# Turning the scan rows of a state-space stage by DMA transposes in place of TensorE transposes

## The reference, cut to what matters

```python
y = ssd(xs, dt, a, bm, cm)                 # chunked scan: diagonal part + carried state
y = y + d_skip[:, None] * xs
y = y.reshape(bsz, s, SSM_D_INNER) * silu(z_ssm)
y = rms_norm(y per group of 512 columns) * ssm_norm_g
y_ssm = y @ w_branch_ssm                   # 2048 -> 1024 columns
merged = sigmoid(g_att) * y_att + sigmoid(g_ssm) * y_ssm
x = x + gate * (merged @ w_out)
```

## Time and profile before

| what | value |
|---|---|
| median of 3 runs | 2744.04 us (2742.4 to 2745.33) |
| span of the profiled execution | 2738.7 us |
| PE busy in the span | 2476.7 us (90%) |
| DVE busy | 1654.1 us (60%) |
| ACT busy | 1033.5 us (38%) |
| POOL busy | 629.3 us (23%) |
| scan stage of group 0 | about 1958 to 2071 us |
| scan stages of groups 1 to 3, first instruction of DVE | 2150.09, 2341.31, 2532.41 us |

### The profile page before, as it was taken

One profiled execution on the slowest core, in us unless ns is written; L12 is line 12 of the kernel. 1 busy time (PEld: TensorE's weight loads), 2 busy tenths in 40 slices (PEclk: granted clock), 3 DMA queues, 4 the chain that ended last, 5 costly groups with the idle time before them and its releaser, 6 DMA issues. The chain is left out here.

```text
span 2738.7 us, 40825 instructions
## 1 busy us (share of the span) xinstructions
PE 2476.7 (90%) x15855; PEld 1326.7 (48%) x15855; DVE 1654.1 (60%) x2961; ACT 1033.5 (38%) x1594; POOL 629.3 (23%) x618
## 2 busy tenths in 40 slices
PE   4999985989799997699789989898999999999999
PEld 3556543545455554355334446644454444444444
DVE  6787774322233233576499988754774766757864
ACT  5111452221122222555544348822443533624620
POOL 2021020000000001331345410000540731712702
PEclk9999997999899999799899999999999999999999
DMA  8685575899999998220112210053002002011133
GB/s 245 205 290 177 197 268 196 316 386 391 389 386 370 385 350 300 84 70 16 39 39 85 95 52 2 17 208 131 8 1 100 8 1 100 9 52 49 66 116 126
DMA packets 131570, 433.12 MB, mean 158 GB/s; under 512 B 27792, under 2 KB 37392, under 8 KB 122960
## 3 DMA queue, kind: packets, MB, share of 16 engines
q1 hardware_dynamic: 95536, 349.13, 35.0%
q10 hardware_dynamic: 25696, 48.93, 5.0%
q0 software_dynamic: 10176, 32.78, 4.0%
HBM read 371.86 MB, written 58.94 MB: 157 GB/s over the span
## 5 line engine op out<-in xcount | busy, mean ns | idle before, releaser
L1484 PE MATMUL m_gu<-conv_y,m_xT 128*64 128x256 f32 x1024 | 233.6, 388 | 17.8 <-DMA arena<-in_moe_w_up 15.5
L2604 POOL TENSOR_TENSOR group_words<-group_words 128x1024 f16<-128x1024 f16 x64 | 149.8, 2361 | 373.7 <-PE i_pj L144 364.4
L1486 PE MATMUL m_gu<-arena,m_xT 128*64 128x256 f32 x1024 | 233.6, 388 | 0.0
L1563 DVE TENSOR_TENSOR m_hid<-m_sg,m_gu 64x256 f32<-64x256 f32 x96 | 39.6, 412 | 318.2 <-ACT m_sg L1532 318.2
L1486 PEld LDWEIGHTS m_gu<-arena,m_xT 128*64 128x64 f32 x1024 | 143.1, 140 | 73.9 <-issue 15.4
L1532 ACT ACT_TABLE_LOAD x48 | 61.6, 1283 | 305.8 <-issue 293.1
L1506 PE MATMUL m_y_ps<-arena,m_hidT 128*64 128x512 f32 x768 | 175.4, 598 | 0.0
L1484 PEld LDWEIGHTS m_gu<-conv_y,m_xT 128*64 128x64 f32 x1024 | 143.1, 140 | 36.0 <-issue 25.0
L142 PE MATMUL s_pj<-hT,arena 128*128 128x512 f16 x384 | 147.4, 384 | 12.7 <-issue 11.6
L142 PE MATMUL i_pj<-hT,group_words 128*128 128x512 f16 x384 | 146.5, 381 | 13.5 <-DVE group_words L357 8.0
L143 PE MATMUL s_pj<-hT,arena 128*128 128x512 f16 x384 | 147.1, 383 | 0.0
(11 more groups left out here) (594 smaller groups left out, 6634.7 us busy)
## 6 DMA issues: line engine op xcount, KB each, us to landing
arena<-in_moe_w_down SPq DMA_DIRECT2D x32, 2048.0 KB, 24.9
conv_y<-in_moe_w_gate SPq DMA_DIRECT2D x22, 2048.0 KB
arena<-in_moe_w_up SPq DMA_DIRECT2D x22, 2048.0 KB
hT<-in_moe_w_gate SPq DMA_DIRECT2D x10, 2048.0 KB
hT<-in_moe_w_up SPq DMA_DIRECT2D x10, 2048.0 KB
x_tok<-in_ada_w ACTq DMA_DIRECT2D x8, 2048.0 KB, 12.6
slot_out<-m_y ACTq DMA_DIRECT2D x96, 128.0 KB
arena<-in_w_gates SPq DMA_DIRECT2D x24, 512.0 KB, 4.2
```

Of the source, the lines that this page charges most:

```text
L1484: g = nc.tensor.matmul(gu_ps[i][g_rows, 0:FFN // 2], lhsT=xT[:, c, :], rhs=k.wg[e % WEIGHT_SLOTS][:, c, cols], start=c == 0, stop=c == KC - 1)
L1486: u = nc.tensor.matmul(gu_ps[i][u_rows, 0:FFN // 2], lhsT=xT[:, c, :], rhs=k.wu[e % WEIGHT_SLOTS][:, c, cols], start=c == 0, stop=c == KC - 1)
L1563: nc.vector.tensor_tensor(hid[:, i, :], sg[:, i, :], gu_ps[i][u_rows, 0:FFN // 2], ALU.mult) \
L2604: return tuple(k.nc.gpsimd.tensor_tensor(k.y_U[:, t % 2, n], k.adt_parts[:, n, t, heads].unsqueeze(2).to_broadcast([P, HPG, P]), k.upto16. ...
```

## The change

ACT and DVE now make the two f16 parts of each row before it is turned, for the rows 0 to 6. They lie in the chunk's 512 f32 words of `x_ssm`, which are no longer needed then: 512 f16 columns of high part, 512 of low part. SP turns such a row with one DMA transpose of 128 x 1024 f16 straight into `yT`. Row 7 is still turned on TensorE and split after it. In the last group SP issues the merge loads behind its seven transposes.

```diff
+        rows16 = lambda t: k.x_ssm[:, t, :].bitcast(F16).rearrange("p (a n) -> p a n", a=2)
+        turned_in = [k.sem(f"y{g}_turned_in{i}") for i in range(2)]
...
+        def turn_rows(sp, t):
+
+            sp.wait_ge(q["row_low"], t + 1)
+            sp.dma_start_transpose(yT.rearrange("p a c s -> p (a c) s")[:, :, t * P:(t + 1) * P],
+                                   rows16(t).rearrange("p a n -> p (a n)")).then_inc(turned_in[t // 4], 16)
+
         if g + 1 == SSM_GROUPS:
...
                 sp.wait_ge(k.att_stored, 16 * KC)
+                for t in range(TT - 1):
+                    turn_rows(sp, t)
                 sp.wait_ge(q["z_done"], TT - EARLY_Z)
...
+                sp.wait_ge(turned_in[0], 16 * 4)
+                sp.wait_ge(turned_in[1], 16 * 3)
...
-            def transposes(t):
-
-                pe.wait_ge(q["normed"], t + 1)
-                if t:
-                    pe.wait_ge(q["tr_low"], t)
+            def last_turn():
+                pe.wait_ge(q["normed"], 1)
                 for c in range(4):
-                    last = nc.tensor.transpose(tr[:, c * P:(c + 1) * P], k.z_ssm[:, t, c * P:(c + 1) * P],
+                    last = nc.tensor.transpose(tr[:, c * P:(c + 1) * P], k.z_ssm[:, TT - 1, c * P:(c + 1) * P],
...
-                if j == 0 or j == KC:
-                    pe.wait_ge(q["tr_high"], 4 + a // P)
-                    pe.wait_ge(q["tr_low"], 4 + a // P)
+                if j == 0:
+                    pe.wait_ge(turned_in[0], 16 * 4)
+                elif j == KC:
+                    pe.wait_ge(turned_in[1], 16 * 3)
+                    pe.wait_ge(q["tr_high"], 1)
+                    pe.wait_ge(q["tr_low"], 1)
...
-                if t >= 2:
-                    transposes(t - 2)
+                if t == TT + 1:
+                    last_turn()
...
-                if t >= 2:
-                    act.wait_ge(q["tr_done"], t - 1)
-                    nc.scalar.copy(yT[:, 0, :, (t - 2) * P:(t - 1) * P],
-                                   tr[:, :].rearrange("p (c q) -> p c q", q=P)).then_inc(q["tr_high"], 1)
+                    if t < TT:
+                        act.wait_ge(q["rstd"], t)
+                        nc.scalar.activation(rows16(t - 1)[:, 0], k.z_ssm[:, t - 1, :], ACT.Copy,
+                                             scale=ss[:, t - 1:t]).then_inc(q["row_high"], 1)
...
-                if t - 1 in end:
-                    accumulate(dve, end[t - 1])
...
-                    step(v.reciprocal(ss[:, t - 1:t], ss[:, t - 1:t]))
+                    v.reciprocal(ss[:, t - 1:t], ss[:, t - 1:t]).then_inc(q["rstd"], 1)
+                if t == TT:
+                    dve.wait_ge(q["rstd"], TT)
                     v.tensor_scalar(k.z_ssm[:, t - 1, :], k.z_ssm[:, t - 1, :], ss[:, t - 1:t], None, ALU.mult) \
...
-                if t >= 2:
-                    dve.wait_ge(q["tr_high"], t - 1)
-                    h = yT[:, 0, :, (t - 2) * P:(t - 1) * P]
-                    v.tensor_tensor(yT[:, 1, :, (t - 2) * P:(t - 1) * P],
-                                    tr[:, :].rearrange("p (c q) -> p c q", q=P), h, ALU.subtract) \
-                        .then_inc(q["tr_low"], 1)
...
+                if t in end:
+                    accumulate(dve, end[t])
+                if 1 <= t < TT:
+                    dve.wait_ge(q["row_high"], t)
+                    v.scalar_tensor_tensor(rows16(t - 1)[:, 1], in0=k.z_ssm[:, t - 1, :], scalar=ss[:, t - 1:t],
+                                           in1=rows16(t - 1)[:, 0], op0=ALU.mult, op1=ALU.subtract) \
+                        .then_inc(q["row_low"], 1)
```

More of the change, by code:

```diff
@@ L2845, in ssm_scan_stage @@
         tr, br = k.ps(f"y{g}_tr", [P, HALF], ctx=ctx), k.ps(f"y{g}_br", [P, HALF], ctx=ctx)
+        rows16 = lambda t: k.x_ssm[:, t, :].bitcast(F16).rearrange("p (a n) -> p a n", a=2)
+        turned_in = [k.sem(f"y{g}_turned_in{i}") for i in range(2)]
         names = ("pool_in", "U_done", "seg_done", "cb_done", "E_done", "cbm_done", "M_done", "yd_done",
-                 "yo_done", "st_done", "state_done", "yo_read", "y_done", "gated", "squared", "std", "normed",
-                 "tr_done", "tr_high", "tr_low", "br_done", "br_out", "dve_step", "xd_done", "f_high", "f_low",
+                 "yo_done", "st_done", "state_done", "yo_read", "y_done", "gated", "squared", "std", "rstd",
+                 "row_high", "row_low", "normed", "tr_done", "tr_high", "tr_low", "br_done", "br_out", "dve_step", "xd_done", "f_high", "f_low",
                  "small", "z_done", "z_out")
@@ L3029, in _ @@
                                          scale=1.0 / GW).then_inc(q["std"], 1)
-                if t >= 2:
-                    act.wait_ge(q["tr_done"], t - 1)
-                    nc.scalar.copy(yT[:, 0, :, (t - 2) * P:(t - 1) * P],
-                                   tr[:, :].rearrange("p (c q) -> p c q", q=P)).then_inc(q["tr_high"], 1)
+                    if t < TT:
+                        act.wait_ge(q["rstd"], t)
+                        nc.scalar.activation(rows16(t - 1)[:, 0], k.z_ssm[:, t - 1, :], ACT.Copy,
+                                             scale=ss[:, t - 1:t]).then_inc(q["row_high"], 1)
+                if t == TT + 1:
+                    act.wait_ge(q["tr_done"], 1)
+                    nc.scalar.copy(yT[:, 0, :, (TT - 1) * P:], tr[:, :].rearrange("p (c q) -> p c q", q=P)) \
+                        .then_inc(q["tr_high"], 1)
             if g + 1 < SSM_GROUPS:
@@ L3101, in _ @@
                     dve.wait_ge(q["std"], t)
-                    step(v.reciprocal(ss[:, t - 1:t], ss[:, t - 1:t]))
+                    v.reciprocal(ss[:, t - 1:t], ss[:, t - 1:t]).then_inc(q["rstd"], 1)
+                if t == TT:
+                    dve.wait_ge(q["rstd"], TT)
                     v.tensor_scalar(k.z_ssm[:, t - 1, :], k.z_ssm[:, t - 1, :], ss[:, t - 1:t], None, ALU.mult) \
                         .then_inc(q["normed"], 1)
-                if t >= 2:
-                    dve.wait_ge(q["tr_high"], t - 1)
-                    h = yT[:, 0, :, (t - 2) * P:(t - 1) * P]
-                    v.tensor_tensor(yT[:, 1, :, (t - 2) * P:(t - 1) * P],
-                                    tr[:, :].rearrange("p (c q) -> p c q", q=P), h, ALU.subtract) \
-                        .then_inc(q["tr_low"], 1)
-            accumulate(dve, end[TT + 1])
+                if t == TT + 1:
+                    dve.wait_ge(q["tr_high"], 1)
+                    v.tensor_tensor(yT[:, 1, :, (TT - 1) * P:], tr[:, :].rearrange("p (c q) -> p c q", q=P),
+                                    yT[:, 0, :, (TT - 1) * P:], ALU.subtract).then_inc(q["tr_low"], 1)
+                if t in end:
[5 more added lines that the diff above has]
+                        .then_inc(q["row_low"], 1)
             for j in range(KC, 2 * KC):
```

## The result

The changed kernel takes 2754.66 us (median of 4 runs, 2752.74 to 2759.44), the kernel before 2743.61 beside it on the same chip: ratio 1.0044, 95% interval 1.0032 to 1.0056. So it is slower, by 11 us, where the forecast had 5.5. The profiled execution has a span of 2750.8 us, 12.1 above that of before. The stages ahead of the scan differ by a few us from execution to execution, so what follows goes by strides: from the first instruction of a group's scan stage on DVE (the memset of `eps`) to that of the next. Before, a stride is 191.1; after, 194.3. Each group pays 3.2 us.

The account below looks back on a forecast made before the run. The prediction took the ring of DVE and POOL, not TensorE, as the bound: +1.08 + 1.27 - 0.98 = +1.37 per group, +5.5 over four, 2749.5 us. Its own range was 2746 to 2753, the stated range 2736 to 2760.

Parts of the forecast that it names:

- four turns longer by 0.27: DVE's new operation costs 0.45, the dropped L3103 saves 0.18; four turns from chunk 1 to 5 add 1.08 us per group.
- L3088 (before: L3070) late in turn 5: In turn 5 DVE's state decay ends at 5.31 instead of 4.04 after y, making the first accumulate 1.27 us later.
- transposes of rows 5 and 6: Two sets of transposes on TensorE's dense path behind the second branch product go, gaining 2 x 0.49 = 0.98 us per group.
- the clock: TensorE's added idle time was charged nothing, since waits of 1.3 us stand in the trace before.
- The ring of DVE and POOL: In the scan turns DVE and POOL hand one shared resource to and fro, which sets the 10.09 us turn, not TensorE.
- The price of 0.45: Hold on the shared resource by DVE's new operation with two SBUF inputs, 0.45 us, bounds 0.18 and 0.60.
- The round trip over ACT: DVE waits each turn for ACT's 0.73 us copy; the delay is hidden in turns 1 to 4, not in turn 5.
- The transposes of turns 2 to 6: Five sets on TensorE before the second branch product turn into waiting for POOL's operand and the first accumulate: nothing gained.
- The new operation gets in ahead of L2616: Rival, chance 0.17: ACT's copy takes under 0.6 us, turn 5 costs 0.27, a group +0.37, time 2745.5.
- Rows land late: Rival, chance 0.16: from 8.3 us a DMA on, product 8 waits for row 6; 2753.5 at 8.8, near 2763 at 10.
- The ring shrinks: Rival, chance 0.12: the new operation holds nothing from POOL, five turns lose 0.18 each; -7.5 us, 2736.5.
- TensorE is the bound after all: Rival, chance 0.10: removing seven sets of transposes and the 1.3 us wait gains 4.7 us per group, time 2725.

Follow-up runs that it names:

- third run: Changed kernel with a memset to zero in place of the operation making the low parts of rows 0 to 6: 2743.66 us, ratio 1.0004 to the kernel before.
- second run: Changed kernel with row 4's low part computed in turn 6 behind the first accumulate, not in turn 5: 2740.93 us, ratio 1.0004 to the kernel before.
- sixth run: Changed kernel with branch products 1 and 3 put into the accumulator bank that the transposes left idle: 2738.33 us, ratio 0.9985 to the kernel before.
- ninth run: Changed kernel with idle bank used, row 4's low part later, and three filler passes behind the stage's last product: 2731.65 us, ratio 0.9965 to the kernel before.
- first run: Changed kernel with 18 unused TensorE passes filling the wait before product 1: 2750.99 us, ratio 1.0033 to the kernel before.
- seventh: Changed kernel with products 1 and 3 in the idle bank and row 4's low part behind the first accumulate: 2735.40 us, ratio 0.9970 to the kernel before.
- tenth: Repeat of the changed kernel with idle bank and later row 4, without filler passes: 2735.07 us, ratio 0.9977 to the kernel before.
- fourth run: Kernel before, with six added DVE operations ahead of each group's first accumulate and no DMA transposes: 2760.17 us, ratio 1.0071 to the kernel before.
- eighth: Changed kernel with 18 filler passes before product 1 and three behind the stage's last product: 2748.57 us, ratio 1.0014 to the kernel before.

## Why the prediction was right or wrong

Per group, the prediction's terms against the trace of the changed kernel:

| term | predicted | measured |
|---|---|---|
| four turns longer by 0.27 | +1.08 | 4 x 0.27 = +1.08 |
| L3088 (before: L3070) late in turn 5 | +1.27 | +1.27; both together +2.34 at the first accumulate |
| transposes of rows 5 and 6 | -0.98 | -0.92 (L2992 to the last accumulate: 39.04 against 39.96) |
| the clock | 0 | +1.58 (1.69 in the groups 1 to 3) |
| end of the stage | not charged | +0.17 (DVE's wait for all engines 1.29 against 1.12, TensorE's 2.00 against 1.82) |
| sum | +1.37 | +3.17 |

The measured terms are those of group 0. Four times 3.17 is 12.7; the spans differ by 12.1, the medians by 11.

**Right.** The ring of DVE and POOL sets the turn: 10.36 with the new operation, 9.91 without it (third run), 10.09 before. The price of 0.45 for an operation that has two SBUF inputs (L2617 behind it takes 1.49 and not 1.04), its place behind L2616 and the end of L3088 at 5.31 came out to 0.01. The round trip over ACT costs in turn 5 and nowhere else; the second run, which undoes it there alone, gets the loss back. The transposes of turns 2 to 6 bring nothing, because behind them TensorE waits for the accumulate.

**Wrong: "I charge nothing for the clock".** The argument was that waits of 1.3 us stand in the trace before without harm. But the step added up TensorE's idle time turn by turn and did not add it where it gathers. Two of its own results meet in front of product 1. The accumulate comes 2.34 later, and TensorE gets there 0.98 earlier by stage time (2029.67 - 4.01 here, 2027.72 - 0.69 before). It starts the segments of that turn 1.07 later, because the turns are longer, but from there to product 1 it needs 2.05 less, most of it the 1.3 us wait of the earlier trace rows and one set of transposes, which are gone. 0.69 + 2.34 + 0.98 = 4.01, the wait in the trace. This one wait, not the idle time per turn, is what had to be held against the rows. Nothing in the trace before bore on 4 us in this stage, but behind the last scan stage, at the beginning of the merge, it shows the clock falling behind shorter waits, 1.81 and then 2.44 us. TensorE in order of time, then the stretch of the slow passes:

```profile
2650.06 0.38 PE L142 MATMUL mg_ps<-mg_ws,mg_merged 128*128 128x512 f16 x1 [2.44 <-DVE mg_merged L3224]
...
2651.84 0.63 PE L143 MATMUL mg_ps<-mg_ws,mg_merged 128*128 128x512 f16 x1
```

```profile
2651.00:2656.00 5.00, 5.00 (x17) 1.92 (x16) 4.93 (x8) 2.28 (x4) 0.00 (x0) 0.66 0.90 327
```

So the cost had to be bounded: from 0 up to the product run wholly at the lower level, an estimate of 2.60 more. The measured 1.58 lies inside; with it the sum would have been +2.95 a group and 2755.8. That the measured 2754.66 lies inside the stated range of 2736 to 2760 all the same is luck: the forecast's own range ended at 2753, and what reaches beyond it was meant for rows that land late.

**The rivals.** *The new operation gets in ahead of L2616:* no, the copy takes 0.72 and not under 0.6. *Rows land late:* no; 3.0 us, below the lower bound of 4.7 and the 4 to 8 that were named as a sign of being right, and product 8 doesn't wait. The estimate of 10.5 us a row that I had worked out from the Trainium skill (VectorE: DVE Perf Modes, The three transpose paths: 1309 ns for a 128 x 128 block by DMA) falls with it: eight blocks in one instruction land in 3.0 us, 0.38 a block, so that figure must not be multiplied by the number of blocks. *The ring shrinks:* no, but it does when the operation is left out. *TensorE is the bound after all:* no; it waits 1.12 us for L2604 in each of two turns and 4.01 before product 1.

**The merge loads** come behind the seven transposes without harm: they are issued from 2627.19 to 2631.21 and land in a median of 5.8 us instead of 4.7, and the merge doesn't wait for them.

**Open.** Why the change of stage takes 0.17 more is not shown; I tried nothing for it. Nor is shown what decides whether the clock falls behind a wait of 1 to 2.6 us. No run gives the kernel before the three filler passes, so what they would be worth without the change is not known.

## What to carry to other kernels

Work taken off an engine that isn't the bound becomes waiting, and the waiting gathers at that engine's next dependence: add the time by which it arrives earlier to the time by which its input comes later, and hold that one wait against the waits that the trace shows to be harmless. If the moved work leaves a buffer idle (here an accumulator bank), use it to let the engine run past that dependence: with that alone the change that had cost 11 us came out 5.6 us below the kernel before by the medians (sixth run; by the ratio 0.9985, 4 us), and with the moved operation and the filler passes 9 us (ninth run). In a ring in which two engines take turns on a resource, put an operation that needs the resource where the other engine has nothing queued: one operation per group, moved, was worth nearly the whole loss.

## What the runs showed of the hardware

- Whether the granted clock falls behind a wait doesn't hang on that wait's length alone. In front of product 1 it never fell behind waits of up to 1.84 us (kernel before, second run), fell in 3 of 4 groups behind 2.56, and in all behind 3.45 and 4.0 (4 and 8 groups). At the changes of stage between the groups it never fell behind 1.35 or 1.82; behind 2.0 it fell three times of three in the first run, once of three in the second, seventh and tenth, and never in the changed kernel (six times) or in the third and sixth run. At the beginning of a scan stage, behind waits of only 0.94 and 1.09, it fell once in the fourth and the sixth run and twice in the eighth, and in none of the other 44 stages. Most of these falls were worth 1.6 to 1.7 us in a dense stretch, eight or nine passes 0.43 apart instead of 0.22; the largest cost 2.5 us (product 1 of group 0, fourth run).
- Filling one wait can move the fall to another: in the first run it came at the end of the stage instead and cost the same, and in the eighth, with that filled too, it came at the beginning of the stage in two of four groups.
- One DMA transpose of 128 x 1024 f16 from SBUF to SBUF (256 KB) takes 1.23 us to issue and lands in 3.0, sooner than the plain load of 512 KB from DRAM in 4.7.
- An operation on DVE whose second SBUF input is f16 and whose scalar comes from SBUF still takes turns with POOL: it ended 0.54 behind L2616, as L3070 did in the earlier trace rows with 0.55.
